# Six feed-forwards of a float32 transformer kernel: from three block-product pairs of units to four, with none of the units 3 to 10 left plain

## Chip, cores and metric

The kernel runs on one core of a Trainium2 chip. The metric is the device time of one execution in microseconds (us). Matrix products run on TensorE (PE in the profile, its weight loads PEld), elementwise work on VectorE (DVE) and ScalarE (ACT); GpSimd (POOL) does small side work, and SyncE (SP) issues the loads of the weights.

## What is computed

The reference is four encoder layers (feed-forward, mixer, feed-forward, each followed by a layer norm) and then a fifth block of another kind, on 256 tokens of width 1024, all in float32. The change touches only the feed-forward of the four layers:

```python
def swiglu(x, w13, w2):                    # x 256x1024, w13 1024x5632, w2 2816x1024
    gate, up = jnp.split(x @ w13, 2, axis=-1)
    return (jax.nn.silu(gate) * up) @ w2
...
for i in range(DEPTH):                     # DEPTH = 4
    x = layer_norm(ALPHA * x + 0.5 * swiglu(x, ffn1_w13[i], ffn1_w2[i]), ln_g[i, 0], ln_b[i, 0])
    ...                                    # mixer, layer_norm
    x = layer_norm(ALPHA * x + 0.5 * swiglu(x, ffn2_w13[i], ffn2_w2[i]), ln_g[i, 2], ln_b[i, 2])
```

## The kernel before, in words

**Split operands.** Every float32 operand is taken apart into a high part of type fp32r (a copy by ACT: `split_hi`, L529, or `form_high`, L1094) and a low part, value minus high part (a subtraction by DVE: `split_lo`, L536, or `form_low`, L1775). A product is three matmuls: high by high, high by low, low by high (`mm3`, L695 to L697).

**Units of weights.** Weights come in units of 128x2048 float32 (1 MB), through a ring of six slots. SP loads a unit (L503 for the two halves of an up unit, L505 for a down unit) once the unit six places ahead of it in the order has been used. The low part is written over the raw weights.

**A feed-forward** has eleven steps i = 0 to 10 (FIT = 11), each for 256 hidden features. A step has two up units (first and second half of the 1024 input features, gate and up columns side by side) and one down unit. A plain step costs PE 2 halves x 2 token tiles x 4 blocks x 3 = 48 matmuls of 512 columns for up; then four 128x128 transposes of the gated rows (`gturn`, L2445) and 24 matmuls of 512 columns for the down product of the step before it. DVE makes three low parts of 128x2048, two gated tiles (`gate_rows`, L1763) and the low part of the turned tile (`gated_low`, L1769).

**A pair** takes the steps q and q+1 together. The 2x2 block product (two halves of the input features, two steps, two token tiles) is made by seven block products in place of eight, a Winograd form: `paired` on PE (L2397) issues seven `product` calls of 12 matmuls, three of them on weights as loaded, the others on sums of weights or on sums of rows of x. PE then does the down products of q-1 and q, with the two `gturn` between. The sums of weights cost DVE and ACT: four sums (L1797, L1801, L1814, L1817), four high parts (L1094) and four low parts (L1775) of 128x2048, and three combinations of 128x512 results (L1823, L1826, L1831, with four copies from PSUM by ACT, L1098). The first two sums and their high and low parts (`form_1`, `form_2`) are made ahead of the pair, in `before_pair` (L1792), during the plain step q-1. The units of a pair, from v on, stand in the order up(q+1) first half, up(q) first half (never split by itself), up(q) second half, up(q+1) second half, down(q-1), down(q).

**Which steps.** `PAIRED = (3, 6, 9)` (L32): pairs (3,4), (6,7), (9,10), and the steps 0, 1, 2, 5 and 8 are plain. Six of the eight feed-forwards are so; the first of layer 0 and the second of layer 3 have no pairs.

**Order of work.** Every engine runs its own instruction stream in program order, and a semaphore wait holds all that is behind it. What DVE does for a pair is, in order: sum L1814, low part, sum L1817, low part of L1814's sum, low part, low part of L1817's sum, combination L1823, low part, combination L1826, two gates, combination L1831, low part, two gates, `gated_low(q)`, two low parts, `gated_low(q+1)`, one low part. Ahead of `dn(q)`, the down product of q, PE waits for `gated_low(q)` (`gl_ready`); ahead of its fifth product it waits for the low part of L1814's sum (`form_lo`, third of the pair). After the last pair comes the tail (L2528 to L2556), where step 10's down product waits for `gated_low(10)` (L2537), and then the layer norm: bn_stats (L1578, L1584) on DVE, a power on POOL, xn on ACT and DVE (L1599), and its transposes on PE (`turn_norm`, L2352), which stand in PE's stream before the last down products.

Of the kernel before, what the change touches and what calls it, by code (L numbers as in the profile page):

```python
# [28 lines left out]
DH = 64  # L29
DFF = 2816  # L30
FIT = DFF // 256
PAIRED = (3, 6, 9)  # L32
DFF2 = 4096
QL, KVL, RP = 384, 256, 32
MD = DH + RP
# [232 lines left out]
def build(nc, a, out, plan, n_units):  # L268
    T = tables()
    with ExitStack() as ctx:  # L270
# [5 lines left out]
        def sem(name):  # L276
            if name not in sems:
                sems[name] = ctx.enter_context(nc.semaphore(name))
            return sems[name]
# [77 lines left out]
        form_1 = nc.alloc_sbuf_tensor_at("form_1", [P, W], F32, offset=heads_at)  # L357
# [5 lines left out]
        form_2l = nc.alloc_sbuf_tensor_at("form_2l", [P, W], F32R, offset=cx_at)  # L363
# [167 lines left out]
        def split_lo(dve, v):  # L531

            for u, n in units_to("lo", v):
                w = widths[u]
                dve.wait_ge(sem("hi_ready"), u + 1)
                dve.tensor_tensor(lo(u)[:, 0:w], raw[:, (slot[u] + 1) % SLOTS, 0:w], hi(u)[:, 0:w].bitcast(F32),  # L536
                                  ALU.subtract).then_inc(sem("lo_ready"), n)
# [127 lines left out]
        def raw_of(u):  # L665

            return raw[:, (slot[u] + 1) % SLOTS, :]
# [311 lines left out]
        def _(act):  # L979
# [19 lines left out]
            for st in plan:  # L999
# [73 lines left out]
                if kind == "ffn":  # L1073
                    A, D = ffn_units(st)
                    pairs = st["pairs"]

                    def silu(i, t, src):

                        if i:
                            act.wait_ge(sem("g_made"), b("g_made", 0) + 2 * i - 1 + t)  # L1080
                        act.activation(sg[:, t, :], src, ACT.Silu).then_inc(sem("silu_done"), 1)  # L1081

                    def gated_high(i):

                        act.wait_ge(sem("gt_done"), b("gt_done", 0) + i + 1)
                        if i >= 2:
                            act.wait_ge(sem("unit_used"), D(i - 2) + 1)
                        c = 2 * (i % 2)
                        act.activation(oh[:, c:c + 2, :], ps[:, 6, :].rearrange("p (c s) -> p c s", c=2), ACT.Copy).then_inc(sem("gh_ready"), 1)  # L1089

                    def form_high(n, f, dst, src):

                        act.wait_ge(sem("form_made"), b("form_made", 0) + 4 * n + f)
                        act.activation(dst[:, :], src[:, :], ACT.Copy).then_inc(sem("form_hi"), 1)  # L1094

                    def keep(n, k, bank):

                        act.activation(term[k][:, :], ps[:, bank, :], ACT.Copy).then_inc(sem("term_kept"), 1)  # L1098

                    def paired(q):  # L1100

                        n, v = pairs.index(q), A(q + 1)
                        split_hi(act, v + 2)
                        act.wait_ge(sem("unit_used"), v + 1)
                        keep(n, 0, 5)
                        split_hi(act, v + 3)
                        act.wait_ge(sem("form_used"), b("form_used", 0) + 3 * n + 1)
                        keep(n, 1, 7)
                        form_high(n, 3, hi(v + 1), raw_of(v + 1))
                        act.wait_ge(sem("form_used"), b("form_used", 0) + 3 * n + 2)  # L1110
                        keep(n, 2, 5)
                        form_high(n, 4, form_4h, form_2)
                        split_hi(act, v + 4)
                        act.wait_ge(sem("unit_used"), v + 3)
                        keep(n, 3, 5)
                        act.wait_ge(sem("block_made"), b("block_made", 0) + 3 * n + 1)
                        silu(q, 0, term[2][:, 0:256])
                        act.wait_ge(sem("block_made"), b("block_made", 0) + 3 * n + 2)
                        silu(q, 1, term[1][:, 0:256])
                        split_hi(act, v + 5)  # L1120
                        act.wait_ge(sem("block_made"), b("block_made", 0) + 3 * n + 3)
                        silu(q + 1, 0, term[0][:, 0:256])
                        act.wait_ge(sem("form_used"), b("form_used", 0) + 3 * n + 3)
                        silu(q + 1, 1, ps[:, 5, 0:256])
                        gated_high(q)
                        split_hi(act, v + 7)
                        gated_high(q + 1)
                        split_hi(act, v + 8)

                    for i in range(FIT):  # L1130
                        if i - 1 in pairs:
                            continue
                        if i in pairs:
                            paired(i)
                            continue
                        if i + 1 in pairs:
                            split_hi(act, A(i + 2))
                            form_high(pairs.index(i + 1), 1, form_1h, form_1)
                        elif i or ahead[u] == 2:
                            split_hi(act, A(i) + ahead[u])  # L1140
                        if i and i + 1 not in pairs:
                            split_hi(act, A(i) + 1 + ahead[u])
                        if i == 2 and pairs:
                            act.wait_ge(sem("rows_made"), b("rows_made", 0) + 1)
                            act.activation(rows_h[:, :, :, :], rows_s[:, :, :, :], ACT.Copy).then_inc(sem("rows_hi"), 1)
                        if u == 0 and i in (5, 6, 7):
                            steps(i - 5)
                        for t in range(NT):
                            if t == 0:
                                act.wait_ge(sem("h0_done"), b("h0_done", 0) + whole(st, i))  # L1150
                            else:
                                act.wait_ge(sem("unit_used"), A(i) + 2)
                            silu(i, t, ps[:, 4 + t, 0:256])
                            if t == 0 and i + 1 in pairs:
                                form_high(pairs.index(i + 1), 2, form_2h, form_2)
                            if i == 0 and t == 0:
                                split_hi(act, A(0) + ahead[u])
                        if i == 0:
                            split_hi(act, A(0) + 1 + ahead[u])
                        if 0 < i < FIT - 1 and i + 1 not in pairs:  # L1160
                            split_hi(act, D(i - 1) + ahead[u])
                        gated_high(i)
                    split_hi(act, D(FIT - 2) + ahead[u])
# [333 lines left out]
        def _(dve):  # L1497
# [73 lines left out]
            for st in plan:  # L1571
# [182 lines left out]
                if kind == "ffn":  # L1754
# [3 lines left out]
                    def gate_rows(i, t, up):  # L1758

                        dve.wait_ge(sem("silu_done"), b("silu_done", 0) + 2 * i + t + 1)  # L1760
                        if i and t == 0:
                            dve.wait_ge(sem("gt_done"), b("gt_done", 0) + i)
                        dve.tensor_tensor(gt[:, t, :], sg[:, t, :], up, ALU.mult).then_inc(sem("g_made"), 1)  # L1763
# [25 lines left out]
                        dve.wait_ge(sem("rows_hi"), b("rows_hi", 0) + 1)  # L1789
                        tt(rows_l[:, :, :, :], rows_s[:, :, :, :], rows_h[:, :, :, :].bitcast(F32), ALU.subtract).then_inc(sem("rows_lo"), 1)  # L1790

                    def before_pair(q):  # L1792

                        n, v, made = pairs.index(q), A(q + 1), b("form_made", 0) + 4 * pairs.index(q)
                        landed(dve, v)
                        landed(dve, v + 1)
                        tt(form_1[:, :], raw_of(v + 1), raw_of(v), ALU.add).then_inc(sem("form_made"), 1)  # L1797
                        split_lo(dve, v)
                        landed(dve, v + 2)
                        dve.wait_ge(sem("form_made"), made + 1)  # L1800
                        tt(form_2[:, :], raw_of(v + 2), form_1[:, :], ALU.add).then_inc(sem("form_made"), 1)  # L1801
                        gate_rows(q - 1, 0, ps[:, 4, 256:512])
                        form_low(n, 1, form_1l, form_1, form_1h)
                        gate_rows(q - 1, 1, ps[:, 5, 256:512])
                        if q == 3:
                            row_lows()
                        form_low(n, 2, form_2l, form_2, form_2h)
                        gated_low(q - 1)

                    def paired(q):  # L1810
# [23 lines left out]
                        gate_rows(q + 1, 0, term[0][:, 256:512])  # L1834
                        dve.wait_ge(sem("form_used"), use + 3)
                        gate_rows(q + 1, 1, ps[:, 5, 256:512])
                        gated_low(q)
                        split_lo(dve, v + 7)
                        gated_low(q + 1)
                        split_lo(dve, v + 8)  # L1840

# [1493 lines left out]
```

## Time and profile before

| | before |
|---|---|
| time of the unprofiled runs, median of 3 | 2465.41 us (2463.21 to 2465.69) |
| time of the profiled execution | 2466.14 us |
| its span, first to last instruction | 2464.2 us |
| mean granted TensorE clock | 0.996 of full speed |
| PE busy | 2410.9 us, 98% of the span |
| DVE busy | 1852.3 us, 75% |
| ACT busy | 1319.6 us, 54% |
| POOL busy | 409.4 us, 17% |
| DMA | 418.1 MB, 170 GB/s |

Busy time is the time in which an engine has at least one instruction under way. Matmuls overlap: a matmul of 512 columns is listed with about 0.39 us, but the next one starts before it ends, so what counts is the distance between starts. It is similar on DVE: the next instruction can start slightly before the listed end of the one in front.

### The profile page before, as it was taken

The page shows a single profiled execution, that of the slowest core. Times are in us where ns is not written, and L with a number is a line of the kernel's source. Part 1 is how long each engine was busy: PE and PEld are TensorE (multiplying, and loading weights), DVE is VectorE, ACT ScalarE, POOL GpSimd, SP SyncE. Part 2 cuts the span into 40 slices and gives each one's busy share as a digit, 9 for nine tenths or more (in the row PEclk, how much of TensorE's full clock was granted, in tenths as well). Part 3 has the DMA queues.
Part 4 walks back from the last instruction along what each step waited for, and adds up shares of the span by engine and source line. Part 5 has one row for each costly group of instructions (what it writes and reads, how often), then busy time and mean ns, then how long its engine had stood idle before and what let it go on. Part 6 is the DMA issues. An engine that isn't in the chain of part 4 may idle for free. (4 is left out here: it accounts for less than half of the span.)

```text
span 2464.2 us, 32871 instructions
## 1 busy us (share of the span) xinstructions
PE 2410.9 (98%) x13023; PEld 2027.1 (82%) x13023; DVE 1852.3 (75%) x2384; ACT 1319.6 (54%) x1637; POOL 409.4 (17%) x463
## 2 busy tenths in 40 slices
PE   9999999999999999999989999999999998999999
PEld 7888878888888888888878888888878876998998
DVE  5466679889875798898768888887675667897554
ACT  5444555555664556556556655664553355444442
POOL 0002310000001100000230000001359602580000
PEclk9999999999999999999999999999999999999999
DMA  8555445656554465565515565565445542336553
GB/s 273 188 187 156 143 146 190 204 171 200 193 172 137 137 197 196 177 199 188 167 58 184 188 209 171 187 206 158 133 149 191 189 153 71 116 124 205 171 188 111
DMA packets 313945, 418.10 MB, mean 170 GB/s; under 512 B 18761, under 2 KB 271042, under 8 KB 313794
## 3 DMA queue, kind: packets, MB, share of 16 engines
q1 hardware_dynamic: 313794, 416.01, 51.8%
q8 instruction: 105, 1.72, 0.3%
q14 instruction: 46, 0.38, 0.1%
HBM read 414.92 MB, written 1.05 MB: 169 GB/s over the span
## 5 line engine op out<-in xcount | busy, mean ns | idle before, releaser
L536 DVE TENSOR_TENSOR wlo<-raw,whi 128x2048 fp32r<-128x2048 f32 (+1 forms) x370 | 861.4, 2341 | 159.0 <-ACT whi L529 158.2
L529 ACT ACTIVATE whi<-raw 128x2048 fp32r<-128x2048 f32 (+1 forms) x375 | 700.4, 1887 | 6.0 <-DMA raw<-in_ffn_w_dram 3.1
L695 PE MATMUL ps<-whi,xh 128*128 128x512 f32 (+2 forms) x1367 | 510.8, 374 | 7.9 <-DVE wlo L1647 2.2
L697 PE MATMUL ps<-whi,xl 128*128 128x512 f32 (+2 forms) x1367 | 503.5, 368 | 0.0
L696 PE MATMUL ps<-wlo,xh 128*128 128x512 f32 (+2 forms) x1367 | 503.1, 368 | 0.0
L695 PE MATMUL ps<-whi,oh 128*128 128x512 f32 x944 | 380.1, 403 | 0.0
L697 PE MATMUL ps<-whi,ol 128*128 128x512 f32 x944 | 369.0, 391 | 0.0
L696 PE MATMUL ps<-wlo,oh 128*128 128x512 f32 x944 | 367.9, 390 | 0.0
L695 PEld LDWEIGHTS ps<-whi,xh 128*128 128x128 f32 x1367 | 258.0, 189 | 56.8 <-issue 11.9
L697 PEld LDWEIGHTS ps<-whi,xl 128*128 128x128 f32 x1367 | 257.9, 189 | 43.2
L696 PEld LDWEIGHTS ps<-wlo,xh 128*128 128x128 f32 x1367 | 258.2, 189 | 41.0
L882 POOL TENSOR_TENSOR rstd<-ve,mhalf 128x1 f32<-128x1 f32 x26 | 18.8, 723 | 1476.5 <-DVE ve L1591 1295.2
L697 PEld LDWEIGHTS ps<-whi,ol 128*128 128x128 f32 x944 | 177.1, 188 | 38.8
L695 PEld LDWEIGHTS ps<-whi,oh 128*128 128x128 f32 x944 | 177.5, 188 | 34.3 <-issue 2.1
L696 PEld LDWEIGHTS ps<-wlo,oh 128*128 128x128 f32 x944 | 177.8, 188 | 32.7
L1081 ACT ACTIVATE sg<-ps 128x256 f32<-128x256 f32 x122 | 46.4, 380 | 219.0 <-PE ps L697 216.7
L695 PE MATMUL ps<-xh,whi 128*128 128x256 f32 (+2 forms) x496 | 138.5, 282 | 1.0 <-DVE wlo L536 1.0
L696 PE MATMUL ps<-xl,whi 128*128 128x256 f32 (+2 forms) x496 | 136.0, 277 | 0.0
L697 PE MATMUL ps<-xh,wlo 128*128 128x256 f32 (+2 forms) x496 | 136.0, 277 | 0.0
L1089 ACT ACTIVATE oh<-ps 128x512 fp32r<-128x512 f32 x88 | 52.7, 599 | 145.6 <-PE ps L2445 145.6
L1763 DVE TENSOR_TENSOR gt<-sg,ps 128x256 f32<-128x256 f32 x122 | 50.9, 418 | 105.9 <-ACT sg L1081 103.4
L695 PEld LDWEIGHTS ps<-xh,whi 128*128 128x128 f32 (+2 forms) x496 | 91.9, 185 | 3.1 <-DVE wlo L536 1.7
(412 smaller groups left out, 3988.8 us busy)
## 6 DMA issues: line engine op xcount, KB each, us to landing
raw<-in_ffn_w_dram SPq DMA_DIRECT2D x350, 512.0 KB, 4.9
raw<-in_ffn_w_dram SPq DMA_DIRECT2D x88, 1024.0 KB, 5.0
raw<-in_w_ff_dram SPq DMA_DIRECT2D x32, 1024.0 KB, 5.4
raw<-in_w_out_dram SPq DMA_DIRECT2D x20, 1024.0 KB, 4.9
raw<-in_w_in_dram SPq DMA_DIRECT2D x20, 1024.0 KB, 5.1
raw<-in_dsa_w_in_dram SPq DMA_DIRECT2D x32, 512.0 KB, 4.6
raw<-in_dsa_w_in_dram SPq DMA_DIRECT2D x12, 1024.0 KB, 5.1
raw<-in_fox_w_in_dram SPq DMA_DIRECT2D x16, 512.0 KB, 5.0
```

The costliest lines, as they stand in the source:

```text
L529: act.activation(hi(u)[:, 0:w], raw[:, (slot[u] + 1) % SLOTS, 0:w], ACT.Copy).then_inc(sem("hi_ready"), n)
L536: dve.tensor_tensor(lo(u)[:, 0:w], raw[:, (slot[u] + 1) % SLOTS, 0:w], hi(u)[:, 0:w].bitcast(F32), ALU.subtract).then_inc(sem("lo_ready"), n)
L695: pe.matmul(o, ah, bh, start=start, stop=False, skip_group_check=True)
L696: pe.matmul(o, ah, bl, start=False, stop=False, skip_group_check=True)
L697: return pe.matmul(o, al, bh, start=False, stop=stop, skip_group_check=True)
L882: pool.tensor_tensor(rstd[:, t, 0:1], ve[:, t, 0:1], mhalf[:, 0:1], ALU.pow).then_inc(sem("rstd_ready"), 1)
L1081: act.activation(sg[:, t, :], src, ACT.Silu).then_inc(sem("silu_done"), 1)
L1089: act.activation(oh[:, c:c + 2, :], ps[:, 6, :].rearrange("p (c s) -> p c s", c=2), ACT.Copy).then_inc(sem("gh_ready"), 1)
L1763: dve.tensor_tensor(gt[:, t, :], sg[:, t, :], up, ALU.mult).then_inc(sem("g_made"), 1)
```

## The change

The pairs are (3,4), (5,6), (7,8), (9,10). For the pairs that have another pair right behind them, DVE makes the next pair's first sum after the last gate and before `gated_low(q)`, the second one after it, and their low parts around `gated_low(q+1)`; ACT makes the high parts between `gated_high(q)` and `gated_high(q+1)`. `before_pair` is cut in two functions so that its sums can be called from there; it stays as it was for the first pair. In the last pair, DVE now makes only one low part (that of step 10's down unit) between `gated_low(9)` and `gated_low(10)`, and two after it. PE's and SP's code is the same, with the other list of pairs.

```diff
-PAIRED = (3, 6, 9)
+PAIRED = (3, 5, 7, 9)
...
                         silu(q + 1, 1, ps[:, 5, 0:256])
+                        if q + 2 in pairs:
+                            split_hi(act, v + 6)
+                            gated_high(q)
+                            form_high(n + 1, 1, form_1h, form_1)
+                            form_high(n + 1, 2, form_2h, form_2)
+                            gated_high(q + 1)
+                            return
                         gated_high(q)
                         split_hi(act, v + 7)
                         gated_high(q + 1)
...
-                    def before_pair(q):
-
-                        n, v, made = pairs.index(q), A(q + 1), b("form_made", 0) + 4 * pairs.index(q)
+                    def two_summed(q):
+
+                        v = A(q + 1)
                         landed(dve, v)
                         landed(dve, v + 1)
                         tt(form_1[:, :], raw_of(v + 1), raw_of(v), ALU.add).then_inc(sem("form_made"), 1)
+
+                    def three_summed(q):
+
+                        n, v = pairs.index(q), A(q + 1)
                         split_lo(dve, v)
                         landed(dve, v + 2)
-                        dve.wait_ge(sem("form_made"), made + 1)
+                        dve.wait_ge(sem("form_made"), b("form_made", 0) + 4 * n + 1)
                         tt(form_2[:, :], raw_of(v + 2), form_1[:, :], ALU.add).then_inc(sem("form_made"), 1)
+
+                    def before_pair(q):
+
+                        n = pairs.index(q)
+                        two_summed(q)
+                        three_summed(q)
                         gate_rows(q - 1, 0, ps[:, 4, 256:512])
...
                         gate_rows(q + 1, 1, ps[:, 5, 256:512])
+                        if q + 2 in pairs:
+                            two_summed(q + 2)
+                            gated_low(q)
+                            three_summed(q + 2)
+                            form_low(n + 1, 1, form_1l, form_1, form_1h)
+                            gated_low(q + 1)
+                            form_low(n + 1, 2, form_2l, form_2, form_2h)
+                            return
                         gated_low(q)
-                        split_lo(dve, v + 7)
+                        split_lo(dve, v + 6 if q + 1 == FIT - 1 else v + 7)
                         gated_low(q + 1)
                         split_lo(dve, v + 8)
```

## Rows read from the trace of the kernel before

**Rows 1.** Part 1 of the page: busy us, share of the span, instructions.
```profile
PE 2410.9 (98%) x13023; PEld 2027.1 (82%) x13023; DVE 1852.3 (75%) x2384; ACT 1319.6 (54%) x1637; POOL 409.4 (17%) x463
```
**Rows 2.** Who PE waited for: us in total, times, longest us.
```profile
PE ps L2537 <- DVE ol L1769: 4.5, 6, 0.8
```
**Rows 3.** Busy by stretch (pair, step 5, steps 3-10): us, PE PEld DVE ACT POOL, PEclk, DMA.
```profile
387.88:419.00 31.12, 31.12 (x142) 25.56 (x141) 27.07 (x21) 19.60 (x19) 0.00 (x0) 1.00 0.62 203
419.00:435.77 16.77, 16.77 (x77) 13.91 (x76) 15.91 (x10) 8.64 (x7) 0.00 (x0) 1.00 0.60 189
387.88:513.00 125.12, 125.12 (x565) 102.82 (x563) 109.35 (x75) 75.63 (x68) 0.00 (x0) 1.00 0.61 200
```
**Rows 4.** PE in order of time: starts of product 1, product 5, dn(3), next step.
```profile
387.88 0.39 PE L695 MATMUL ps<-whi,xh 128*128 128x512 f32 x1
...
398.93 0.39 PE L695 MATMUL ps<-whi,rows_h 128*128 128x512 f32 x1
...
413.06 0.39 PE L695 MATMUL ps<-whi,oh 128*128 128x512 f32 x1
...
419.00 0.39 PE L695 MATMUL ps<-whi,xh 128*128 128x512 f32 x1
```
**Rows 5.** DVE in order of time, pair (3,4): start, duration, what ended idle time.
```profile
387.91 2.28 DVE L1814 TENSOR_TENSOR raw<-raw 128x2048 f32<-128x2048 f32 x1
390.11 2.28 DVE L536 TENSOR_TENSOR wlo<-raw,whi 128x2048 fp32r<-128x2048 f32 x1
...
396.01 2.29 DVE L1775 TENSOR_TENSOR wlo<-raw,whi 128x2048 fp32r<-128x2048 f32 x1 [1.42 <-ACT whi L1094]
...
408.40 2.29 DVE L536 TENSOR_TENSOR wlo<-raw,whi 128x2048 fp32r<-128x2048 f32 x1 [0.79 <-ACT whi L529]
...
410.96 0.41 DVE L1763 TENSOR_TENSOR gt<-sg,ps 128x256 f32<-128x256 f32 x1
411.30 0.68 DVE L1769 TENSOR_TENSOR ol<-ps,oh 128x512 fp32r<-128x512 f32 x1
412.95 4.49 DVE L536 TENSOR_TENSOR wlo<-raw,whi 128x2048 fp32r<-128x2048 f32 x2 [0.98 <-ACT whi L529]
```
**Rows 6.** DVE's groups, whole span: count, busy us, mean ns, idle before.
```profile
L1797 DVE TENSOR_TENSOR form<-raw 128x2048 f32<-128x2048 f32 x18 | 41.1, 2284 | 0.0
L1826 DVE TENSOR_TENSOR term<-term,term 128x512 f32<-128x512 f32 x18 | 12.3, 684 | 0.0
```
**Rows 7.** DVE in order of time, end of the same feed-forward and its norm.
```profile
513.19 0.68 DVE L1769 TENSOR_TENSOR ol<-ps,oh 128x512 fp32r<-128x512 f32 x1
513.79 2.28 DVE L536 TENSOR_TENSOR wlo<-raw,whi 128x2048 fp32r<-128x2048 f32 x1
515.99 0.69 DVE L1578 BATCH_NORM_STATS2 st<-ps 128x6 f32<-128x512 f32 x1
...
518.57 0.81 DVE L1599 TENSOR_SCALAR xn<-ps,rstd,nmr 128x512 f32<-128x512 f32 x1
```
**Rows 8.** PE in order of time there: the wait at L2537, the norm's transposes.
```profile
513.92 0.73 PE L2537 MATMUL ps<-whi,ol 128*128 128x512 f32 x2 [0.76 <-DVE ol L1769]
...
519.40 1.09 PE L2352 MATMUL ps<-ident,xn 128*128 128x128 f32 x8
```
**Rows 9.** Busy time by stretch, columns as in rows 3: around two of PE's stalls.
```profile
1292.00:1296.00 4.00, 2.61 (x21) 1.97 (x21) 1.24 (x2) 2.05 (x2) 1.25 (x1) 1.00 0.84 251
2008.00:2012.00 4.00, 4.00 (x11) 3.11 (x10) 3.78 (x6) 2.70 (x3) 0.07 (x1) 0.50 0.00 0
```
**Rows 10.** PE in order of time, the same two places.
```profile
1293.39 0.52 PE L2780 MATMUL ps<-ident,pr 128*128 128x128 f32 x3 [1.65 <-POOL pr L958]
...
2006.57 0.80 PE L733 MATMUL ps<-whi,xh 128*128 128x512 f32 x1 [2.02 <-ACT xh L1039]
...
2007.59 0.63 PE L733 MATMUL ps<-whi,xh 128*128 128x512 f32 x1
2008.02 0.63 PE L734 MATMUL ps<-wlo,xh 128*128 128x512 f32 x1
```

## The prediction

> **What bounds the kernel now.** I read the page's shares of busy time first: PE is busy 98% of the span, DVE 75% [rows 1]. The list of PE's waits comes next. In the six paired feed-forwards it has one entry that returns in each: PE waits 0.76 us for `gated_low(10)` at L2537, 4.5 us in all [rows 2, 8]. The busy times by stretch then show the eight steps 3 to 10 of one feed-forward: 125.12 us, PE busy for all of it, DVE for 109.35 [rows 3]. So PE bounds the pairs now, and a block product less is worth its full time as long as PE stays fed.
>
> The same rows show how thin the cover is. A pair takes 31.12 us on PE and a plain step 16.77 [rows 3]. DVE is busy 27.07 and 15.91 us of these, and it does much of a pair's work in the plain step ahead of it. What counts on an in-order engine is which of its results is late. In the order of time, DVE starts on L1814 at 387.91, when PE has just started the pair (387.88), and its next instruction starts 2.20 us later, although each is listed with 2.28 [rows 4, 5]. I use 2.20 for every 128x2048 instruction of DVE, 0.60 for a 128x512 one (listed 0.68, less the same 0.08) and 0.345 for a gate.
>
> **What PE saves.** Steps 3 to 10 are three pairs and two plain steps before, 3 x 31.12 + 2 x 16.77 = 126.9 us, and four pairs after, 124.5. That is 2.4 us per feed-forward, 14.5 in the six. The wait at L2537 should go too, as `gated_low(10)` now stands behind one low part and not two: 0.76 x 6 = 4.5 us. SP's loads are the same 33 units in another order. A pair's own units come in the same order and are freed by the same products as before, at the same distance of six, so SP passes nothing new; I cost the loads at nothing, covered by the 4 us and more that lie between landing and use. ACT gets five high parts of weights and four of sums in a pair; it is busy 19.60 of 31.12 us before [rows 3], and the two more of about 1.9 us each leave it room. It has one new wait of note: the high part of the second sum waits for DVE, and `gated_high(q+1)` stands behind it. That makes DVE wait some 0.35 us more in each handover, counted below.
>
> **What DVE has to do in one pair now.** Before, the two first sums, their two low parts and the low part of `up(q+1)`'s first half were spread over a plain step. Now all of it falls within the pair in front. Per pair of 31.12 us of PE, DVE has five low parts of weights, four low parts of sums, four sums: 13 x 2.20 = 28.65; three combinations 1.8; four gates 1.4; two `gated_low` 1.2. Sum 33.05 us. To this come waits that the order of the code forces: 0.79 ahead of the low part of down(q), where ACT's high part comes after a silu that waits for DVE itself [rows 5], 0.2 for the turn-around at L1826 and the gates, and the 0.35 above. DVE's cycle is about 34.4 us, 3.3 longer than PE's. DVE becomes the bound in these stretches.
>
> **Walk through one feed-forward**, with the times of the first. Pair (3,4) begins as before, since `before_pair` and steps 0 to 2 are unchanged. DVE is done with the last gate at 411.30 [rows 5]. Now the sum L1797 comes first, 2.20, and `gated_low(3)` ends at 414.18; PE wants it for dn(3) at 413.06 [rows 4]. First stall, 1.15 us. DVE goes on: low part, sum, low part, 0.35 of waiting, `gated_low(4)`, low part: 411.30 + 5 x 2.20 + 2 x 0.61 + 0.35 = 423.85 before it starts L1814 of the pair (5,6). PE starts that pair at 419.00 + 1.15 = 420.15. DVE began level with PE in pair (3,4) and is 3.7 us behind in this one. Its third instruction ends, and the low part of L1814's sum starts, at 423.85 + 6.61 = 430.46. That one no longer waits the 1.42 us for ACT [rows 5], and is ready at 432.75. PE's fifth product comes 11.05 us into a pair [rows 4], at 431.2. Second stall, 1.6 us. From that low part to the end of the gates DVE needs 411.30 - 396.01 = 15.29 us [rows 5], plus 2.20 for the new sum and 0.68 for `gated_low(5)`: 448.6. PE wants it 14.13 us after product five, at 446.9. Third stall, 1.7 us. Pair (7,8) repeats the last two, pair (9,10) has only the one at product five, because no sum is put ahead of `gated_low(9)`. PE's stalls: 1.15 + 3 x 1.65 + 2 x 1.75 = 9.6 us.
>
> **The exit.** It is simplest in DVE's own time, as DVE now sets it. Before: from L1814 of the first pair (387.91) to bn_stats (515.99) 128.1 us [rows 5, 7]. After: 35.9 to L1814 of pair (5,6); two cycles of 6.61 + 15.29 + 12.55 = 34.45; in pair (9,10) 21.9 to the end of the gates, which is 514.65; `gated_low(9)` 0.6; a low part, with 0.45 of wait for ACT, 2.65; `gated_low(10)` with 0.5 of wait, 1.1; then two low parts where there was one [rows 7], 4.4. That reaches 523.45. Last-but-one low part moved behind `gated_low(10)`: it spares PE the wait at L2537, but bn_stats now stands 1.5 us behind PE's results. From bn_stats to the norm's transposes it is 519.40 - 515.99 = 3.41 us, and PE arrived there just when xn was finished, at 518.57 + 0.81 = 519.38 [rows 7, 8], so nothing absorbs it. DVE and PE both reach that point 523.45 - 515.99 = 7.46 us later. The check from PE's side: 9.6 of stalls - 2.4 saved - 0.76 + about 1.1 new at the transposes = 7.5.
>
> The other five feed-forwards have the same pattern (18 pairs in all, L1797 18 times with 2284 ns [rows 6], six waits at L2537 [rows 2]). Behind the norm, every engine is displaced alike, and a ring of six units holds no more work ahead than before. Sum: 6 x 7.46 = 44.8 us on the profiled execution's 2466.14 us, 2510.9. The profiled execution lies 0.7 us over the median of the runs, so the forecast for the median is 2510.2 us.
>
> **Bounds of what no row shows.** (a) The order of DVE's stream leaves ACT's answers (0.35, 0.45, 0.5) unseen; at nothing the time is 6 x 2.0 = 12 us less, at twice their size 12 more. Nearest is the 0.79 and 0.98 us that DVE waits for ACT's high parts in rows 5; I take the values as they fall out of the walk. (b) The exit: if bn_stats' lag is covered by something, 1.0 us of each feed-forward goes, 2504. (c) A floor for DVE: the change adds eight instructions of 128x2048 and takes away one low part, 7 x 2.20 = 15.4 us, and three combinations (684 ns each [rows 6]), 1.8; DVE was idle for 125.12 - 109.35 = 15.8 us of the stretch [rows 3]. Were all of that idle time filled, steps 3 to 10 would still last 109.35 + 17.2 = 126.6 us, 1.4 more than before.
>
> **Rivals.**
> A, PE stays the bound (faster). The 14.5 us of matmuls and the 4.5 us at L2537 are gained and DVE's extra work finds room: 2465.4 - 19 = 2446. For it: PE 98%, DVE 75% over the span, and ACT, which DVE waits for in each pair, has room. It decides if DVE's cycle is under 31.1 us. Against it: 33.05 us of work alone, without a wait. Chance 0.05.
> B, DVE is the bound, but with its idle time filled (floor (c)): +1.4 per feed-forward, 8 to 9 us, 2474. Against it: the idle time of the first pair (1.42 at L1775) and of the tail stays where it is. Chance 0.07, with 0.03 of it inside 0.2%.
> C, as forecast but with the exit covered, 2504. Chance 0.15.
> D, TensorE's clock falls. What rows show: after a lone stall of 1.65 us the granted clock stayed at 1.00 (2.4 GHz) [rows 9, 10]; about 2004, where PE stood still for over 4 us in two pieces around eight transposes, it went to 0.50 (1.2 GHz), matmuls started 0.43 us apart instead of 0.23, and it was back about 5 us later [rows 9, 10], some 2.3 us lost. In the changed kernel stalls of 1.1 to 1.8 us come some 14 us apart. If the clock fell at each, PE would lose 4.6 us in a pair with two of them; 3.4 of these would have been stall anyway, so 1.2 per cycle, and with what isn't covered at the first pair and at the exit 4 us per feed-forward: 2535. Chance 0.04. The Trainium skill, page "TensorE: Matmul & The Clock Gate", section "A second HAM failure mode: psum-queue depth-cycling", has such a rule: engine stops that are short but come between every group of matmuls make the clock swing between half and full. No run here shows it at these distances.
> The forecast itself: 0.69.
>
> **How the numbers follow.** The forecast is the likeliest case. The range takes in C and the bounds of (a) up to 2522: 2490 to 2522, which leaves out A, B, D and the outer edges, about 2 in 10. A measurement of this kernel can tell 0.2%, 5 us, from no change. Faster by more: A, 0.05. Within: part of B, 0.03. Slower: 0.92.
>
> **What would show it.** In the changed profile, step by step: PE's waits have `ol` L1769 (1.1 to 1.8 us, 18 times, three per feed-forward) and `wlo` L1775 (about 1.65 us, 18 times) as their largest entries, some 60 us in all, and none at L2537. A pair (5,6) takes 34.5 us from product one to the next, with PE busy under 32 of it, DVE busy over 32. L1814 of pair (5,6) starts 3.7 us after PE's product one, not level. L1775 of L1814's sum waits for ACT only in the first pair. The granted clock stays at 1.00 in the pairs. The forecast is wrong if PE is busy throughout the pairs (A), if the distance from L1814 to L1814 is under 34 us (B), if bn_stats doesn't follow straight on a low part (C), or if matmuls 0.43 us apart appear in a pair (D).

## The result, and the profile after

The changed kernel takes 2510.94 us (median of four runs, 2509.59 to 2511.00), the kernel before 2464.31 us (2462.60 to 2465.69, four runs). The ratio is 1.0185, with a 95% interval of 1.0173 to 1.0197: slower by 46.6 us. The profiled execution took 2509.59 us, with a span of 2507.8 us.

Part 1 of the page of the changed kernel, and the longest of PE's waits (us in total, times, longest):

```profile
PE 2403.0 (96%) x12951; PEld 2010.0 (80%) x12951; DVE 1953.2 (78%) x2444; ACT 1365.0 (54%) x1679; POOL 411.4 (16%) x463
```

```profile
PE ps L695 <- DVE ol L1776: 25.0, 18, 1.6
PE ps L695 <- DVE wlo L1782: 21.9, 18, 1.2
PE ps L2377 <- ACT xn L1005: 10.9, 12, 1.6
```

PE has 72 matmuls fewer than before [rows 1], 12 for each feed-forward, and waits for DVE in two places that had no wait before: 18 times for a turned tile's low part (`gated_low`) and 18 times for the low part at product five. The third row is the norm's transposes, which wait for xn; six of its twelve waits, 1.5 to 1.6 us each, are new. L2537's wait [rows 2] is gone from the list.

Two stretches of the first feed-forward, each as long as one pair now lasts (columns as in rows 3). They begin 0.5 us ahead of the first matmul of pair (5,6), which starts at 420.70; those of (7,8) and (9,10) start at 455.13 and 489.56, 34.43 us apart:

```profile
420.15:454.60 34.45, 31.73 (x142) 25.43 (x141) 33.34 (x23) 21.38 (x20) 0.00 (x0) 1.00 0.57 183
454.60:489.10 34.50, 31.78 (x142) 25.44 (x141) 33.39 (x23) 21.41 (x20) 0.00 (x0) 1.00 0.55 184
```

A pair took 31.12 us with PE busy throughout [rows 3]; it now takes 34.45, with DVE busy for 33.34 of it and PE for 31.73. The granted clock is 1.00. DVE in order of time shows why:

```profile
388.23 2.28 DVE L1831 TENSOR_TENSOR raw<-raw 128x2048 f32<-128x2048 f32 x1
...
411.62 2.28 DVE L1804 TENSOR_TENSOR form<-raw 128x2048 f32<-128x2048 f32 x1
413.82 0.68 DVE L1776 TENSOR_TENSOR ol<-ps,oh 128x512 fp32r<-128x512 f32 x1
...
421.37 0.69 DVE L1776 TENSOR_TENSOR ol<-ps,oh 128x512 fp32r<-128x512 f32 x1 [0.26 <-ACT oh L1089]
421.98 2.28 DVE L1782 TENSOR_TENSOR form_2l<-form,form_2h 128x2048 fp32r<-128x2048 f32 x1
424.18 2.29 DVE L1831 TENSOR_TENSOR raw<-raw 128x2048 f32<-128x2048 f32 x1
...
430.78 2.29 DVE L1782 TENSOR_TENSOR wlo<-raw,whi 128x2048 fp32r<-128x2048 f32 x1
...
458.60 2.28 DVE L1831 TENSOR_TENSOR raw<-raw 128x2048 f32<-128x2048 f32 x1
...
518.84 0.69 DVE L1776 TENSOR_TENSOR ol<-ps,oh 128x512 fp32r<-128x512 f32 x1 [0.45 <-ACT oh L1089]
519.45 4.49 DVE L536 TENSOR_TENSOR wlo<-raw,whi 128x2048 fp32r<-128x2048 f32 x2
523.85 0.69 DVE L1585 BATCH_NORM_STATS2 st<-ps 128x6 f32<-128x512 f32 x1
```

L1831 is the line that was L1814 [rows 5]. From one of them to the next DVE takes 424.18 - 388.23 = 35.95 us in the first pair and 458.60 - 424.18 = 34.42 us in the second, in which it waits only 0.78 us (ahead of the low part of the down unit, as before) and 0.26 us. PE's first matmul of pair (5,6) starts 3.48 us before DVE's L1831 does. PE's stalls in the same feed-forward, one row each (the bracket is the idle time ahead):

```profile
414.65 0.47 PE L695 MATMUL ps<-whi,oh 128*128 128x512 f32 x1 [1.10 <-DVE ol L1776]
...
433.12 0.50 PE L695 MATMUL ps<-whi,rows_h 128*128 128x512 f32 x1 [1.20 <-DVE wlo L1782]
...
449.07 0.47 PE L695 MATMUL ps<-whi,oh 128*128 128x512 f32 x1 [1.51 <-DVE ol L1776]
...
527.26 1.09 PE L2377 MATMUL ps<-ident,xn 128*128 128x128 f32 x8 [1.56 <-ACT xn L1005]
```

### The profile page after: what moved, and what is told of

It is laid out like the page before. It is cut to its first block and busy times, and to the rows that moved or that the text cites. A ratio compares the mean times of both kernels' runs of the same rounds, so it can differ in the third digit from the quotient of the medians.

```text
span 2507.8 us, 32889 instructions
## 1 busy us (share of the span) xinstructions
PE 2403.0 (96%) x12951; PEld 2010.0 (80%) x12951; DVE 1953.2 (78%) x2444; ACT 1365.0 (54%) x1679; POOL 411.4 (16%) x463
## 5 line engine op out<-in xcount | busy, mean ns | idle before, releaser
L536 DVE TENSOR_TENSOR wlo<-raw,whi 128x2048 fp32r<-128x2048 f32 (+1 forms) x364 | 849.2, 2343 | 138.7 <-ACT whi L529 137.7
L529 ACT ACTIVATE whi<-raw 128x2048 fp32r<-128x2048 f32 (+1 forms) x369 | 691.7, 1887 | 6.8 <-DMA raw<-in_ffn_w_dram 4.0
L695 PE MATMUL ps<-whi,xh 128*128 128x512 f32 (+2 forms) x1223 | 454.7, 372 | 7.5 <-DVE wlo L1654 2.2
L697 PE MATMUL ps<-whi,xl 128*128 128x512 f32 (+2 forms) x1223 | 447.6, 366 | 0.0
L696 PE MATMUL ps<-wlo,xh 128*128 128x512 f32 (+2 forms) x1223 | 447.4, 366 | 0.0
L695 PEld LDWEIGHTS ps<-whi,xh 128*128 128x128 f32 x1223 | 231.0, 189 | 51.1 <-issue 11.6
L697 PEld LDWEIGHTS ps<-whi,xl 128*128 128x128 f32 x1223 | 231.0, 189 | 37.7
L696 PEld LDWEIGHTS ps<-wlo,xh 128*128 128x128 f32 x1223 | 231.1, 189 | 35.4
L1098 ACT ACTIVATE term<-ps 128x512 f32<-128x512 f32 x96 | 57.5, 599 | 81.6 <-PE ps L697 81.6
L695 PE MATMUL ps<-whi,rows_h 128*128 128x512 f32 x192 | 77.5, 404 | 21.9 <-DVE wlo L1782 21.9
```

The costliest lines, as they stand in the source:

```text
L529: act.activation(hi(u)[:, 0:w], raw[:, (slot[u] + 1) % SLOTS, 0:w], ACT.Copy).then_inc(sem("hi_ready"), n)
L695: pe.matmul(o, ah, bh, start=start, stop=False, skip_group_check=True)
L696: pe.matmul(o, ah, bl, start=False, stop=False, skip_group_check=True)
L697: return pe.matmul(o, al, bh, start=False, stop=stop, skip_group_check=True)
```

## The experiments

Ten kernels ran. Times are medians, and the ratios are to the kernel before on the same chip (2465 to 2466 us in each set of runs). The theory is that of the prediction: DVE's work per pair, and not where it stands, sets the pace.

### Order or amount: `gated_low(q)` first

```diff
-                            two_summed(q + 2)
                             gated_low(q)
+                            two_summed(q + 2)
```

> The changed kernel with gated_low(q) ahead of the next pair's first sum (three places per feed-forward). Theory (DVE's work per pair, 34.4 us, sets the pace; order doesn't matter): the waits for ol L1776 go (25.0 us in the changed kernel), but what is saved there comes back at product five, so the time stays within 2 us of the changed kernel's 2510.9 us. Rival (the late gated_low is the loss, because the sum was put ahead of it): 18 stalls of 1.4 us go, 2486 us.

Measured 2509.5 us, ratio 1.0178 (1.0161 to 1.0195), the changed kernel's time. PE's longest waits in it:

```profile
PE ps L695 <- DVE wlo L1782: 24.3, 18, 1.4
PE ps L695 <- DVE wlo L536: 23.1, 20, 1.4
```

The 25.0 us of waiting for `gated_low` are gone, and 23.1 us of waiting for an L536 low part stand in their place, at product four (two of the 20, 1.0 us in all, stand elsewhere, in the changed kernel too). I had expected them at product five alone. The total doesn't move: the stall goes to whatever DVE makes next.

### Taking DVE work away, and adding some

One sum less (and the next with both): the pairs with another pair in front of them work on a weight unit as loaded where the sum belongs, so part of the result is another. The lines shown are from the first of the two runs, shortened; the second run leaves out the `form_2` sum in the same way.

```diff
-                        tt(form_1[:, :], raw_of(v + 1), raw_of(v), ALU.add).then_inc(sem("form_made"), 1)
+                        n = slice(0, W if q == 3 else 1)
+                        tt(form_1[:, n], raw_of(v + 1)[:, n], raw_of(v if q == 3 else v + 1)[:, n], ALU.add).then_inc(sem("form_made"), 1)
...
-                            form_high(n + 1, 1, form_1h, form_1)
+                            form_high(n + 1, 1, form_1h, raw_of(v + 7))
```

> The changed kernel without the next pair's first sum at the three handovers of a feed-forward (the pair then works with a weight unit as loaded in place of the sum, so that part of the result is another one): 2.2 us less of DVE work per handover. Theory: DVE's cycle falls to 32.2 us, still over PE's 31.1; 6.4 us less per feed-forward, 38 in all, 2473 us. Rival (late gated_low is the loss): only its 25 us go, 2486 us.

Measured 2470.8 us, ratio 1.0020 (1.0010 to 1.0030). One of PE's two waits is gone and the other is smaller, at product five:

```profile
PE ps L695 <- DVE wlo L1782: 13.5, 18, 0.9
```

> The changed kernel without both first sums at the handovers (weight units as loaded in their place, another result): 4.4 us less of DVE work per handover. Theory: DVE's cycle is 30.0 us and PE's 31.1, so PE is the bound again: no stall in the pairs, 9.7 us less per feed-forward at the norm's transposes than in the changed kernel, 2452 us, and not the 2435 us of a straight line through the run with one sum less. Rival (the clock or another cost of adjacent pairs on PE): stalls stay and it is over 2465.

Measured 2452.4 us, ratio 0.9947 (0.9927 to 0.9967). The stretch from 420 to 480 us of that run, with one pair and most of another:

```profile
420.00:480.00 60.00, 60.00 (x272) 49.29 (x271) 56.07 (x44) 41.21 (x38) 0.00 (x0) 1.00 0.65 209
```

PE is busy for all of it. The first sum taken away is worth 2510.9 - 2470.8 = 40.1 us, 2.23 us for each of the 18 handovers, which is one 128x2048 instruction in full; in the profiles DVE's cycle from pair to pair falls from 34.42 to 32.29 us. The second is worth 18.4 us, 1.0 us each, because PE's own 31.1 us is reached on the way: the cycle is 31.11 us. So four pairs would gain 13.7 us if DVE had two such instructions less to do in each handover.

One sum more:

```diff
+                        if q > 3:
+                            ch.step(tt(form_1[:, :], raw_of(v + 1), raw_of(v), ALU.add))
                         tt(form_1[:, :], raw_of(v + 1), raw_of(v), ALU.add).then_inc(sem("form_made"), 1)
```

> The changed kernel with the next pair's first sum made twice at the handovers: 2.28 us more of DVE work in each. Theory: every microsecond is paid in full, 6.8 us per feed-forward, 41 in all, 2552 us. Rival B (DVE's idle time fills first): DVE waits 1.3 us per cycle for ACT in the changed kernel, and with these filled it would be about 24 us less than that, 2528 us.

Measured 2561.1 us, ratio 1.0388 (1.0367 to 1.0409): 9 us more than expected, 0.5 for each handover. The stall at `gated_low` has become long, and PE comes out of it slower. Rows of PE, then a stretch (columns as in rows 3), then DVE in the pair behind it:

```profile
417.49 0.76 PE L695 MATMUL ps<-whi,oh 128*128 128x512 f32 x1 [3.40 <-DVE ol L1776]
418.06 0.63 PE L696 MATMUL ps<-wlo,oh 128*128 128x512 f32 x1
418.48 0.63 PE L697 MATMUL ps<-whi,ol 128*128 128x512 f32 x1
```

```profile
418.00:422.00 4.00, 4.00 (x11) 3.07 (x10) 4.00 (x3) 0.91 (x2) 0.00 (x0) 0.50 0.08 33
```

```profile
434.24 2.29 DVE L1782 TENSOR_TENSOR wlo<-raw,whi 128x2048 fp32r<-128x2048 f32 x1 [0.53 <-ACT whi L1094]
```

Matmuls start 0.42 to 0.43 us apart, not 0.23, and the granted clock is 0.50 (1.2 GHz). PE's early products are late, ACT's copies wait for them, and DVE, which had no gap at this line in pair (5,6) of the changed kernel, waits 0.53 us for ACT. The 18 stalls differ, and that allows a comparison within the run. Behind ten of them, 11 or 12 matmuls run at the slow pace, and DVE waits at L1782 in the next pair in all ten cases, 0.26 to 0.58 us. Behind the other eight, at most 8 matmuls are slow, and DVE doesn't wait there in any. One of the eight has no slow matmul, though its stall is as long:

```profile
1448.92 0.47 PE L695 MATMUL ps<-whi,oh 128*128 128x512 f32 x1 [3.43 <-DVE ol L1776]
```

```profile
1449.00:1453.00 4.00, 4.00 (x20) 3.32 (x21) 4.00 (x2) 1.13 (x1) 0.00 (x0) 1.00 0.19 77
```

The ten waits are 5.0 us in all. Ahead of the low part of step 10's down unit DVE waits 0.98 us for ACT in place of 0.53, 2.7 us in the six feed-forwards; whether the slow clock causes that is not shown. The rest of the 9 us is in part the sum made twice, which takes 0.1 us more than 2.20. This is rival D's mechanism: real behind 17 of 18 stalls of 3.4 to 3.8 us, absent behind the 1.1 to 1.6 us of the changed kernel.

### Number of handovers, not of pairs

```diff
-PAIRED = (3, 5, 7, 9)
+PAIRED = (3, 5, 8)
```

> The changed kernel's code with PAIRED = (3, 5, 8): pairs (3,4), (5,6), then step 7 plain, pair (8,9), step 10 plain. As many pairs and plain steps as before, so PE's matmuls are as many, but one handover from pair to pair per feed-forward. Theory (each handover lets DVE fall 3.3 us behind PE, a plain step, 16.8 us on PE and 11 to 13 on DVE, gives it back): two stalls per feed-forward, 1.1 at gated_low(3) and 1.2 to 1.6 at product five of pair (5,6), none in pair (8,9); 2.5 us x 6 = 15 us over the kernel before, 2480 us, give or take 4 for a last step that is plain. Rival (a plain step doesn't refill DVE): stalls in pair (8,9) too, 2490 us or more.

Measured 2479.4 us, ratio 1.0056 (1.0041 to 1.0072). PE's waits:

```profile
PE ps L695 <- DVE wlo L1782: 7.3, 6, 1.2
PE ps L695 <- DVE ol L1776: 6.6, 6, 1.1
```

Six of each, one handover's worth in each of six feed-forwards, 13.9 us for 13.6 us of difference. In the first feed-forward they stand at 412.46 and 430.93, and none is in pair (8,9): the plain step 7 lets DVE catch up. That is what the plain steps of the kernel before do.

### The end of the last pair

The kernel before, with the new order at its last pair:

```diff
-                        split_lo(dve, v + 7)
+                        split_lo(dve, v + 6 if q + 1 == FIT - 1 else v + 7)
                         gated_low(q + 1)
```

> The kernel before (pairs 3, 6, 9) with only the change at the last pair: one low part between gated_low(9) and gated_low(10), two behind it. Theory (DVE sets the time at which the norm's transposes can start, and DVE's work up to there is unchanged): PE's wait at L2537, 0.76 us in six places, goes and comes back ahead of the norm's transposes; no gain, -1 to +4 us against the kernel before. Rival (the wait at L2537 was a loss of its own, as the prediction counted it): 4.5 us less, 0.2%.

Measured 2471.2 us, ratio 1.0022 (1.0012 to 1.0031): 6 us slower, more than the +4 at the outside of the range. DVE, then PE:

```profile
511.86 0.69 DVE L1769 TENSOR_TENSOR ol<-ps,oh 128x512 fp32r<-128x512 f32 x1 [0.45 <-ACT oh L1089]
512.47 4.49 DVE L536 TENSOR_TENSOR wlo<-raw,whi 128x2048 fp32r<-128x2048 f32 x2
516.87 0.69 DVE L1578 BATCH_NORM_STATS2 st<-ps 128x6 f32<-128x512 f32 x1
```

```profile
520.28 1.09 PE L2352 MATMUL ps<-ident,xn 128*128 128x128 f32 x8 [1.56 <-ACT xn L1005]
```

No wait is left at L2537, but bn_stats starts at 516.87 where it started at 515.99, and the transposes at 520.28 where it was 519.40 [rows 7, 8]. Of these 0.88 us, 0.34 were there when the first pair began (L1814 starts at 388.25, not 387.91). The other 0.54 come from `gated_low(10)`, which, moved forward, must wait 0.45 us for ACT's copy (and starts only after the listed end of the instruction in front, not 0.09 us before it), and DVE pays for that in full: DVE was already the late one here, by itself, in the kernel before. So PE's 0.76 us are not gained, and some 0.5 us are lost in each feed-forward, 3.1 us in the six. The profiled executions differ by 4.2 us and the medians by 6.1; what makes up the rest is open.

With the last low part left to the norm as well:

```diff
                         gated_low(q + 1)
-                        split_lo(dve, v + 8)
+                        split_lo(dve, v + 7 if q + 1 == FIT - 1 else v + 8)
```

> As the run before this one, and the last low part (second unit of the next stage) left to the norm, where it stands behind the first half's xn. Theory: bn_stats comes 2.2 us earlier in DVE's stream, PE loses neither the 0.76 us at L2537 nor time at the norm's first transposes: 1.2 us less per feed-forward, 7 us in all, about 2458 us, less if the low part is late for its new place. Rival: the low part now delays xl and the second half's xn by 2.2 us, and the gain is gone there: within 3 us of the kernel before.

Measured 2461.5 us, ratio 0.9988 (0.9979 to 0.9996). DVE, then PE at the second half's transposes:

```profile
514.94 0.69 DVE L1578 BATCH_NORM_STATS2 st<-ps 128x6 f32<-128x512 f32 x1
...
521.65 2.28 DVE L536 TENSOR_TENSOR wlo<-raw,whi 128x2048 fp32r<-128x2048 f32 x1
```

```profile
527.72 1.06 PE L2352 MATMUL ps<-ident,xn 128*128 128x128 f32 x8 [0.30 <-ACT xn L1005]
```

It is faster than both kernels, by 3.6 us of 2465: half of the 7 us expected. The low part stands ahead of the second half's statistics now, and the transposes there wait 0.30 us. The first half's transposes come 1.22 us earlier than before, counted from the norm in front, as expected, and the second half's only 0.8 us (182.5 us before, 181.7 now). That part of the gain is given back, as the rival had it, but not all.

> The kernel before with only the last low part left to the norm, the order at the last pair as before. Theory: bn_stats is free 2.2 us earlier but PE, which still waits 0.76 us at L2537, is then the later one: at most 0.3 us per feed-forward, 0 to 2 us less than the kernel before. Rival (the later low part alone makes the gain of the run that has both): 3 to 4 us less.

With that second edit alone, 2467.2 us, ratio 1.0009 (1.0000 to 1.0018): no gain, and 1.5 us slower where 0 to 2 us faster was expected. PE's 4.5 us at L2537 are still there, and the gain needs both edits.

The same edit in the changed kernel:

> The changed kernel with the same low part left to the norm. Theory: bn_stats isn't held by it, PE's 1.6 us ahead of the norm's transposes go: 1.8 us less per feed-forward, about 10 us, 2500 us, less what is lost by the later low part. Rival (exit covered by something else): no gain, 2511 us.

Measured 2502.9 us, ratio 1.0157 (1.0142 to 1.0173): 8.1 us less than the changed kernel. So 8 of the 46.6 us can be had back at the exit. What the handovers cost, with the saved matmuls taken off, is the difference between two kernels with the same exit: 2510.9 - 2471.2 = 39.7 us with the new order at the last pair, 2502.9 - 2461.5 = 41.4 us with the late low part as well.

### A sum on GpSimd

```diff
-                        tt(raw_of(v + 1), raw_of(v + 2), raw_of(v + 1), ALU.add).then_inc(sem("form_made"), 1)
+                        dve.wait_ge(sem("third_sum"), b("third_sum", 0) + n + 1)
...
+                        pool.wait_ge(sem("form_made"), b("form_made", 0) + 3 * n + 1)
+                        pool.tensor_tensor(raw_of(v + 1), raw_of(v + 2), raw_of(v + 1), ALU.add).then_inc(sem("third_sum"), 1)
```

> The changed kernel with the sum of L1814 (one of the four of a pair) made by GpSimd, which is idle in these stages, as soon as the first sum is made. DVE has one 128x2048 instruction less per pair. Theory: if DVE keeps its 2.20 us per instruction, its cycle is 32.2 us, six feed-forwards are 37 us shorter, 2474 us. Rival (GpSimd and DVE slow one another, as in the stretch from 1700 to 1900 us of the kernel before, where DVE's low parts took 2.72 us in place of 2.28): over some 7 us of GpSimd per pair DVE loses 1 to 2 us again, 2490 to 2505 us.

Measured 2561.3 us, ratio 1.0392 (1.0378 to 1.0406): worse than either expectation. POOL and DVE at a handover:

```profile
416.85 4.60 POOL L884 TENSOR_TENSOR raw<-raw 128x2048 f32<-128x2048 f32 x1 [35.78 <-DVE form L1814]
```

```profile
417.22 6.37 DVE L536 TENSOR_TENSOR wlo<-raw,whi 128x2048 fp32r<-128x2048 f32 x1
423.52 2.28 DVE L1822 TENSOR_TENSOR form<-raw,form 128x2048 f32<-128x2048 f32 x1
```

The same in the plain step ahead of the first pair, where DVE's low part is under way when GpSimd's sum comes:

```profile
374.32 2.28 DVE L536 TENSOR_TENSOR wlo<-raw,whi 128x2048 fp32r<-128x2048 f32 x1
375.83 5.24 POOL L884 TENSOR_TENSOR raw<-raw 128x2048 f32<-128x2048 f32 x1 [26.55 <-DMA raw<-in_ffn_w_dram]
376.52 6.71 DVE L1822 TENSOR_TENSOR form<-raw,form 128x2048 f32<-128x2048 f32 x1
```

GpSimd makes the sum in 4.60 us. DVE's low part, 2.28 us elsewhere, takes 6.37: 4.1 us more, nearly all of the time that GpSimd was at work after it began. DVE stood still. In the other order it is GpSimd that waits: its sum takes 0.64 us more while the low part ends, and then DVE's next sum is held. The trade is 4.1 us of DVE for 2.2: DVE's cycle from pair to pair is 36.31 us in place of 34.42, 1.9 us worse in each of 18 handovers, 34 of the 50 us that were lost against the changed kernel. The other 16 lie around the six first pairs, where L1822 takes 6.7 us and PE stands still for 2.2 us ahead of the pair, a stall that the changed kernel doesn't have. The Trainium skill, page "SBUF — State Buffer", section "Who interferes with whom", says that a DVE instruction with two SBUF inputs contends with a GpSimd instruction that reads SBUF, and that the one that comes second is blocked altogether. The trace agrees (6.37 us beside 4.60 where DVE came second, 5.24 us in place of 4.60 where GpSimd did).

## Why the prediction was right

The forecast was 2510.2 us, the measurement 2510.94. That the two lie within 0.7 us is partly luck, for the runs of the kernel before alone spread over 3 us. The better test is the added time. Forecast were 7.46 us for each of the six feed-forwards, 44.8 in all; from one norm's transposes to the next they take 7.5 to 7.6 us more, 45.3 in all. The profiled executions differ by less, 43.5 us, as the part behind the sixth came out 2.0 us shorter, and the medians by 46.6. Point by point:

- **What bounds.** "DVE becomes the bound in these stretches": shown by the two runs with one and two sums less, by the swapped order that changed nothing, and by the stretches with DVE busy 33.34 of 34.45 us. The cycle was put at 34.4 us and measured 34.42. (13 x 2.20 is 28.6 and not 28.65, which changes nothing at this precision.)
- **The walk.** L1814 (now L1831) of pair (5,6) was to start 35.94 us after the first one: measured 35.95. bn_stats was to start 523.45 - 387.91 = 135.54 us after it: 523.85 - 388.23 = 135.62. The norm's transposes are 527.26 - 519.40 = 7.86 us later than before, 0.32 of which was there at the start of the first pair; 7.46 was forecast.
- **The stalls of PE.** Forecast 1.15, 1.6 and 1.7 us, measured 1.10, 1.20 and 1.51. The forecast's sizes are distances between starts. The profile's idle time is less, since a matmul that nothing follows shows its full 0.39 us as busy. In distances the stalls of the first feed-forward are 1.26, 1.37 and 1.67 us, and the 36 of the list are 52.8 us, 8.8 per feed-forward, where 9.6 was forecast; as idle time the list has 46.9. The stall at product five was put 0.2 us too long: PE comes to it later than forecast, as the stall ahead is 0.1 us longer and the first matmul behind a stall takes 0.1 us more than the usual 0.23. In the "check from PE's side" that is nearly made up by the transposes, where 1.1 us was forecast and 1.6 measured. The forecast itself went by DVE's time, which these terms don't enter.
- **The two handshakes with ACT** were put at 0.35 and 0.5 us and measured 0.26 and 0.45. The wait ahead of step 10's low part, put at 0.45, was 0.53 in the changed kernel.
- **The exit.** One step was wrong as a step, though not in the sum. "The wait at L2537 should go too: 0.76 x 6 = 4.5 us" names a saving that doesn't exist. The run with only that edit is 6 us slower than the kernel before. The walk had it right further down, because it went on in DVE's time to the transposes; rival A's 2446 us was 4.5 us too low for the same reason. Its matmuls alone, 2465.4 - 14.5 = 2450.9, are close to what the run with two sums less shows (2452.4).
- **Rival B**, idle time filled first, is excluded: an instruction more was paid in full, and one less was earned in full. (Its floor is worked out in a stretch that ends at 513.00, 1.8 us short of the 126.9 us that steps 3 to 10 take.) **Rival C**, exit covered, is excluded by the 8.1 us of the late low part. **Rival D** didn't happen at these stalls, but lies near: 2.2 us more of DVE work per handover was enough to bring it on. The loads, costed at nothing, never hold PE or DVE in either profile.

Not tried: another split of the work between DVE and ACT. What would make four pairs pay is known (two 128x2048 instructions less for DVE in each handover), how to get there isn't.

## What to carry to other kernels

When a cheaper product is paid for with elementwise work, compare the cycles of both engines over the piece that repeats, in distances between starts, with the idle time that the order of the code forces added in. A share of 75% over the whole span said nothing here; 34.4 us of DVE's cycle against 31.1 us of PE's decided it. And follow a removed wait to the next point where both engines meet before it is counted as gained.

## What had not been expected

- GpSimd isn't free help for DVE's two-input instructions: 4.60 us of it cost DVE 4.1 us. The stretch of the kernel before from 1700 to 1900 us, with GpSimd busy for 109.45 of 200 us and low parts at 2.72 us in the mean, had suggested 1 to 2.
- Behind 17 of 18 stalls of 3.4 to 3.8 us TensorE's granted clock is 0.50, for 6 to 12 matmuls; behind the 42 stalls of 1.1 to 1.6 us in and after the pairs of the changed kernel it stays at 1.00. In between lie the six stalls of 2.2 us of the run with the sum on GpSimd: the clock falls at two of them (386.14 and 1417.63 us) and not at the other four. Where DVE sets the pace, the cost that shows is not the slow matmuls themselves, which partly fill what would be the next stall, but the 0.3 to 0.6 us by which they make ACT and so DVE late.
